# Second attention of a two-block transformer kernel: row sums from a column of ones, maxima ahead of VectorE's other work, gate products inside the last unit

## What is computed

```python
def hybrid_layer(x, ...):
    xn = rmsnorm(x, norm_mix)
    (u_rnn, u_gate, q, k_c, v_c, k_s, v_s, k_w, v_w, g_nsa, g_a, g_b) = split(xn @ w_in)
    h_a = rg_lru(causal_depthwise_conv(u_rnn, conv_w, conv_b), ...)
    y_a = h_a * gelu(u_gate)
    y_b = nsa_mixer(q, k_c, v_c, k_s, v_s, k_w, v_w, g_nsa, rel_bias, ...)
    merged = sigmoid(g_a) * (y_a @ proj_a) + sigmoid(g_b) * (y_b @ proj_b)
    h = x + merged @ w_out
    return h + square(relu(rmsnorm(h, norm_mlp) @ w_mlp_in)) @ w_mlp_out

# rg_lru: r, i = sigmoid(block-diagonal products of x); a = exp(-8 r softplus(-lam))
#         h_t = a_t h_{t-1} + sqrt(1 - a_t^2) (i_t x_t)
# nsa_mixer, each of three branches: softmax(q k + bias) v, times a gate, summed
```

## Time and profile before

| | us |
|---|---|
| median of 3 runs | 1597.65 (1597.32 to 1603.59) |
| profiled execution, its own time | 1600.37 |
| its span, first to last instruction | 1598.6 |
| TensorE busy | 1533.4 (96%) |
| VectorE busy | 1030.2 (64%) |
| ScalarE busy | 797.7 (50%) |
| GpSimd busy | 223.3 (14%) |
| mean granted clock of TensorE | 0.984 |

### The profile page before, as it was taken

How to read it: one execution, slowest core, us unless ns; L and a number is a source line. 1 busy time by engine, 2 the same in 40 slices (tenths; PEclk the granted TensorE clock), 3 DMA queues, 4 the chain that set the end, 5 groups by cost and what they waited for, 6 DMA issues and landing times.

```text
span 1598.6 us, 25010 instructions
## 1 busy us (share of the span) xinstructions
PE 1533.4 (96%) x10255; PEld 1381.4 (86%) x10255; DVE 1030.2 (64%) x1704; ACT 797.7 (50%) x1437; POOL 223.3 (14%) x189
## 2 busy tenths in 40 slices
PE   8999999999999999989999999999989799999999
PEld 6899889799987889989889987788877699989887
DVE  5764586787756675578678765555755586666643
ACT  5555454366643455445456653453446664455532
POOL 2300032211102120032031100012010050100000
PEclk9989999999999999999999999999999799999999
DMA  8623255355565533255355555555212144645453
GB/s 310 246 102 99 91 211 185 136 197 183 185 217 189 189 122 118 81 198 185 109 197 180 182 200 178 186 197 185 90 46 76 53 158 157 206 163 184 159 190 123
DMA packets 40353, 258.19 MB, mean 162 GB/s; under 512 B 4512, under 2 KB 5168, under 8 KB 14000
## 3 DMA queue, kind: packets, MB, share of 16 engines
q1 hardware_dynamic: 35600, 238.44, 42.8%
q0 software_dynamic: 2272, 12.57, 2.1%
q10 hardware_dynamic: 2368, 5.58, 0.9%
HBM read 254.98 MB, written 1.07 MB: 160 GB/s over the span
## 4 chain that ended last, share of the span: by engine, by line
PE 73%; DVE 13%; ACT 8%; issue 4%; DMA 2%; POOL 1%; ACTq 0%; POOLq 0%; DVEq 0%; SPq 0%
PE ps L492 65%; DVE lows L1557 5%; ACT wh L1037 3%; PE ps L602 3%; PE ps L683 1%; ACT S L1460 1%; DVE ar L2093 1%; PE ps L704 1%; DMA raw<-d_wst 1%; ACT arR L1538 1%; DVE S L2274 1%; DVE S L2155 1%; DVE xTr L1576 1%; PE ps L722 1%; PE ps L721 0%
## 5 line engine op out<-in xcount | busy, mean ns | idle before, releaser
L1557 DVE TENSOR_TENSOR lows<-raw,wh 128x1024 fp32r<-128x1024 f32 (+3 forms) x473 | 544.9, 1171 | 249.8 <-ACT wh L1037 247.2
L492 PE MATMUL ps<-xTr,wh 128*128 128x256 f32 (+2 forms) x3472 | 633.8, 285 | 3.4 <-DVE S L1924 1.6
L492 PEld LDWEIGHTS ps<-xTr,wh 128*128 128x128 f32 (+2 forms) x3472 | 537.9, 190 | 8.8 <-DVE S L1924 3.0
L1037 ACT CAST wh<-raw 128x1024 fp32r<-128x1024 f32 (+3 forms) x473 | 455.2, 989 | 176.6 <-DMA raw<-d_wst 131.4
L492 PE MATMUL ps<-xTr,lows 128*128 128x256 f32 (+1 forms) x1736 | 491.3, 283 | 0.0
L492 PEld LDWEIGHTS ps<-xTr,lows 128*128 128x128 f32 (+1 forms) x1736 | 330.0, 190 | 0.0
L492 PE MATMUL ps<-wh,arR 128*128 128x512 f32 x928 | 298.2, 399 | 7.4 <-DVE ar L1746 4.0
L492 PEld LDWEIGHTS ps<-wh,arR 128*128 128x128 f32 x928 | 175.1, 189 | 52.7 <-DVE ar L1746 5.7
L492 PE MATMUL ps<-lows,arR 128*128 128x512 f32 x464 | 184.1, 397 | 0.0
L492 PE MATMUL ps<-wh,xTr 128*128 128x512 f32 x480 | 153.3, 397 | 16.7 <-DVE xTr L1576 13.1
L492 PE MATMUL ps<-arR,wh 128*128 128x256 f32 (+1 forms) x832 | 148.7, 281 | 0.0
(11 more groups left out here) (259 smaller groups left out, 1514.7 us busy)
## 6 DMA issues: line engine op xcount, KB each, us to landing
raw<-d_wst SPq DMA_DIRECT2D x196, 1024.0 KB, 4.9
raw<-d_wst SPq DMA_DIRECT2D x24, 512.0 KB, 3.5
raw<-d_wst SPq DMA_DIRECT2D x12, 896.0 KB, 4.5
raw<-d_wst SPq DMA_DIRECT2D x8, 672.0 KB, 4.6
ar<-d_lnp POOLq DMA_DIRECT2D x5, 1024.0 KB, 5.2
raw<-d_wst SPq DMA_DIRECT2D x8, 441.0 KB, 3.5
ar<-d_par POOLq DMA_DIRECT2D x2, 1192.0 KB, 9.6
ar<-d_scr POOLq DMA_DIRECT2D x1, 2048.0 KB, 9.2
```

The costliest lines, as they stand in the source:

```text
L492: op = e.matmul(out, s, m, start=start and i == 0, stop=stop and i == len(pairs) - 1)
L1037: e.copy(high_of(m), raw_of(m)).then_inc(*high.done(m))
L1557: e.tensor_tensor(low_of(m), raw_of(m), high_of(m).bitcast(F32), ALU.subtract).then_inc(*low.done(m))
```

## The change

1. `vb`, the values, gets 65 columns a head (`d=65`); GpSimd sets the 65th to 1 once. `pv2` multiplies by 65 columns, and the sum of a head's probabilities comes out as the 65th column of its result. The exponentials lose their accumulator. VectorE's reciprocal and gate multiplication move from `maxima` into `finish` and read the sum from PSUM.
2. VectorE's order in a unit is now: maxima of unit un, copy of unit un − 1, finish of unit un − 2, two steps (none in unit 0). Its steps thus run one unit behind those of TensorE and ScalarE.
3. In the last unit of tile 1 TensorE runs the gate products (0, 0), (0, 1) and (0, 2) ahead of the last transposes, ahead of the last value product and behind it. ScalarE and VectorE make their halves in units 5 to 7. ScalarE takes their tanh (`gated2`) among the decays and copies that follow.
4. The square root comes behind the tanh of gate product (0, 3), the recurrences start four gate products later, and the splits of their results six iterations behind instead of two, the last two beside `pb`.

```diff
-ARENA = 25360
+ARENA = 25376
-        vb = arena(1024).rearrange("p (i c) -> p i c", i=2)
+        vb = arena(1040).rearrange("p (i h d) -> p i h d", i=2, d=65)
@@ tensor @@
+            def gate2(v, n):
+                features(("g2", v, n), W2, 8, 128, RW, span((GB0, GA0)[v] + n * 128), X, [], act, "g2", v, n)
...
+                    w.wait_ge(pool, "ones")
...
-                            v = br * 256 + h * 64
-                            op = e.matmul(b[:, h * 64:(h + 1) * 64], PTv[:, hold + h, k, :], vb[:, k, v:v + 64],
+                            op = e.matmul(b[:, h * 65:(h + 1) * 65], PTv[:, hold + h, k, :], vb[:, k, 4 * br + h, :],
...
+                if i:
+                    gate2(0, 0)
                 probs_turned(7)
                 lru_next(1)
+                if i:
+                    gate2(0, 1)
                 finish(7)
+                if i:
+                    gate2(0, 2)
@@ scalar @@
+            def gated2(v, n):
+                highs_of("g2", v, n)
+                w.wait_ge(product, "g2", v, n)
+                for k in (6, 7):
+                    w.wait_ge(cross, *(("pv2", 1, k) if v == 0 else ("pT2", 1, k, 1)))
+                e.activation((gb, ga)[v][:, n, :], M["g2", v, n][:, 0:T], ACT.Tanh, scale=0.5).then_inc(*act.done("g2", v, n))
+
+            def branch_high(k):
+                w.wait_ge(pool, "ya", k)
+                e.copy(yaR.h[0:RP, k, :], gg2[0:RP, k, :]).then_inc(*act.done("yah", k))
...
-                        op = e.activation(Sv[:, hold + h, 0:nk], Sv[:, hold + h, 0:nk], ACT.Exp, bias=nb[:, h:h + 1], scale=1.0,
-                                          accum_out=su[:, h:h + 1])
-                        op.then_inc(*act.done("exp2", i, un))
-                    lru_next(2)
+                        e.activation(Sv[:, hold + h, 0:nk], Sv[:, hold + h, 0:nk], ACT.Exp, bias=nb[:, h:h + 1],
+                                     scale=1.0).then_inc(*act.done("exp2", i, un))
+                    lru_next(1 if (i, un) == (1, 7) else 2)
+                    if i and un > 4:
+                        highs_of("g2", 0, un - 5, far=0)
                 probs_copied(7)
-                lru_next(1)
+                if i:
+                    for n in range(2):
+                        gated2(0, n)
+                lru_next(2 if i else 1)
...
+            gated2(0, 2)
             w.wait_ge(cross, "yT", 1, 1)
...
             lru_next(60)
+            gated2(0, 3)
...
+            for n in range(4, 16):
+                gated2(n // 8, n % 8)
+                if n > 5:
+                    branch_high(n - 6)
             for n in range(8):
                 highs_of("pb", n)
+                if n < 2:
+                    branch_high(10 + n)
@@ vector, maxima @@
-                    go = 16 * (br + 1) + 4 * hq
-                    w.wait_ge(act, "exp2", i, un)
-                    e.reciprocal(ri, su).then_inc(*vec.done("ri0", i, un))
-                    w.wait_ge(vec, "ri0", i, un)
-                    e.tensor_tensor(ri, ri, ng[:, i, go:go + 4], ALU.mult).then_inc(*vec.done("ri2", i, un))
@@ vector, finish @@
+                    go = 16 * (un // 4 + 1) + 4 * (un % 4)
+                    o = M["pv2", i, un][:, 0:260].rearrange("p (h d) -> p h d", d=65)
                     w.wait_ge(cross, "pv2", i, un)
+                    e.reciprocal(ri, o[:, :, 64]).then_inc(*vec.done("ri0", i, un))
+                    w.wait_ge(vec, "ri0", i, un)
+                    e.tensor_tensor(ri, ri, ng[:, i, go:go + 4], ALU.mult).then_inc(*vec.done("ri2", i, un))
...
                 for un in range(8):
+                    maxima(un)
                     if un:
                         probs_copied(un - 1)
-                    maxima(un)
+                    if un > 1:
+                        finish(un - 2)
+                    if un:
+                        lru_next(2)
+                    if i and un > 4:
+                        lows_for("g2", 0, un - 5, far=0)
+                probs_copied(7)
+                finish(6)
+                lru_next(1 if i else 3)
+                finish(7)
+                if i:
                     lru_next(2)
-                    if un:
-                        finish(un - 1)
-                probs_copied(7)
-                lru_next(1)
-                finish(7)
+                    lows_for("g2", 0, 3)
...
+            for n in range(16):
+                lows_for("g2", n // 8, n % 8)
+                if n == 4:
+                    w.wait_ge(act, "sqrt")
+                    e.memset(xc[0:RP, :, 0:1], 1.0).then_inc(*vec.done("first"))
+                if n >= 4:
+                    recur(n - 4)
+                if n > 5:
+                    branch_low(n - 6)
@@ gpsimd @@
             e.dma_start(TB, bass.AP(scr_d.tensor, 0, [[1, 128], [384, 16], [1, 256]])).then_inc(*bias_in.done())
+            e.memset(vb[:, :, :, 64:65], 1.0).then_inc(*pool.done("ones"))
```

38 lines of the change are left out of this document (11 added, 27 removed).

## The result

The changed kernel takes 1577.59 us in the median of four runs (1575.99 to 1583.21), the kernel before 1599.87 beside it (four runs); the ratio is 0.9865, with a 95% interval of 0.9831 to 0.9900. The profiled execution took 1578.58 us with a span of 1576.8, so it is 21.8 us shorter than the one of before (1598.6). Forecast were a gain of 22.4 us and a median of 1575.2. The medians differ by 22.3 us; the changed kernel's own lies 2.4 us above the forecast, and 2.2 us of that are the median of before, 1597.65 with three runs when the forecast was made and 1599.87 with four.

A forecast was written before the change was run, and what follows sets the result against it. TensorE, 96% busy, was taken to bound the kernel, with time to win only where it idles in the second attention. Gains 9.0 + 6.3 + 7.4 − 0.3 = 22.4 us off 1597.65 gave 1575.2, range 1570 to 1587.

The forecast's parts named there:

- tile 0: First attention tile: TensorE sets the pace at 7.74 us a unit; 56.0 us against 65.05, gain 9.0 us.
- boundary between the tiles: From tile 0's end to tile 1's first scores: the sum had no term; tile 0's end chain was put at 1.83 us.
- six units of tile 1: Second tile: with the maxima first, units of 6.42 us, six in 38.5 against 44.86; gain 6.3 us.
- last scores to gate product (0,7): Handover to the gate products: 23.4 us against 30.82, less four products already done; idles of 3.5 and 2.4 us; gain 7.4.
- 65th column: 192 value products with 65 columns: 0.3 us lost for all, bounds 0 and 22.
- everything behind: Recurrences, their products on GpSimd and branch splits after the handover keep their pace: nothing won or lost, ±1 us.
- rival B: Clock falls in the new idle before (0,3), which with (0,4) eats the 2.4 us spare: 1577 to 1580; chance 0.12.
- A: Loops hide less, low halves being 0.5 us from late: ten units lose 0.5 us each, 1580; chance 0.12.
- C: Handover gives nothing, ScalarE's queue from last values to square root being longer: gain 15 only, 1582.6; chance 0.09.
- D: No idle before (0,3) because casts run ahead near the square root: 3 to 5 us more, 1571; chance 0.05.
- E: Value products slowed by 65-column rows at odd multiples of four bytes: gain gone if doubled, 1619 if tripled; chance 0.03.
- F: VectorE keeps waiting, for `pv2` instead of `exp2`: 1596 or so; chance 0.04.

The follow-up runs named there:

- e1_sums: Kernel before with only the column of ones and the reciprocal behind the value product, engine order kept: 1600.24 us, ratio 0.9996 to before.
- e9_shift: e1_sums with VectorE's recurrence steps run one unit behind, maxima still after the copy: 1581.71 us, ratio 0.9878 to before.
- e10_first: e1_sums with VectorE's maxima first in each unit and finishing two units later, steps not shifted: 1588.03 us, ratio 0.9921 to before.
- e13_copyfirst: Changed kernel with VectorE's copies ahead of the maxima again and finishing one unit later, steps still shifted: 1576.71 us, ratio 0.9857 to before.
- e2_acc: Changed kernel with the exponentials' accumulators kept, 64 value columns and the reciprocal taken from those sums: 1576.49 us, ratio 0.9852 to before.
- e6_fill: Changed kernel with two unused products of constants on TensorE ahead of the transposes of tile 0's y: 1577.56 us, ratio 0.9851 to before.
- after_again: The changed kernel itself, unaltered, measured again later in six runs: 1576.74 us, ratio 0.9858 to before.
- e11_all: Changed kernel with e5_decays' edits, the cast of (0,7) directly behind the square root, and e6_fill's two products: 1570.83 us, ratio 0.9811 to before.
- e5_decays: Changed kernel with decays 9 to 11 ahead of the gate tanhs, (0,3)'s low half earlier, (0,6)'s cast ahead of the square root: 1572.79 us, ratio 0.9825.
- e4_low: Changed kernel with the low half of gate piece (0,3) made ahead of VectorE's last recurrence steps: 1579.88 us, ratio 0.9865 to before.

## Why the prediction came out right, and where it did not

Term by term, from the two profiled executions:

| term | forecast | measured |
|---|---|---|
| tile 0 | 9.0 | 65.05 − 56.25 = 8.8 |
| boundary between the tiles | 0 | 9.21 − 12.54 = −3.3 |
| six units of tile 1 | 6.3 | 44.86 − 38.52 = 6.3 |
| last scores to gate product (0,7) | 7.4 | 42.5 − 35.3 = 7.2 |
| 65th column | −0.3 | 0 |
| everything behind | 0 | 2.6 |
| rest | 0 | 0.1 |
| sum | 22.4 | 21.8 (rounded) |

**Tile 0: the sum right, its reason wrong.** 56.25 us against 56.0, units of 7.72 to 7.98 against 7.74, the end chain's idle 1.82 against 1.83. TensorE's work does set the pace, as the sum said. But the step "the change takes the wait for the exponentials off VectorE" credits the wrong edit. With that wait alone removed (e1_sums) nothing is gained, because behind it stood the cast that ScalarE makes after the same exponentials; I had both waits in the earlier trace rows, 1.71 and 0.46 us, and subtracted both without asking which edit removes the second. The one that does is the shift of the recurrence steps by a unit (e9_shift), and it makes the first one harmless too. The maxima's place with the later finishing removes a part of it alone (e10_first, 62.06 us).

**Tile 1: the same.** 38.52 against 38.5. "After the change the maxima come first" was to be the reason; e9_shift and e13_copyfirst have them second and take 38.52. By an estimate, 1 us of the 6.3 is the half clock of before at 1246.7 to 1250.1, which made its last scores late: the unit ahead of them took 8.09 us, and 7.05 in e1_sums, whose VectorE keeps the same pace. The handover's gain is smaller by as much.

**The handover: right but for one step.** (0,2) done and y transposed at 1259.17, 16.8 us after the scores, and to 17.5 with the transposes themselves; idle 3.37 against 3.5; (0,3) at 21.2 against 21.0; the square root at 29.7 against 29.8; (0,7) could start at 34.8 against 34.9, and does in e2_acc, e13_copyfirst and e6_fill. The step that went otherwise is rival B's: the clock fell in the new idle, to 0.50 in 1264 to 1268, and (0,3) and (0,4), partly at half clock, ate the 2.4 us that TensorE had to spare ahead of (0,7). In those three kernels 0.4 us of idle are left; in the changed kernel, where half clock lasted longer, none, and (0,7) came 0.5 us late, at 35.3. So B cost 0.5 us here, because the square root's chain is nearly as long. The Trainium skill's page "TensorE: Matmul & The Clock Gate", section "HAM oscillation — how this bites in real kernels", tells of a kernel whose bursts of products, with waits between them, each start at half rate; for the idles of 3.4 to 4.8 us the traces agree, six of six, and for the 1.82 us idle in six cases of eleven.

**The boundary: the step that is missing.** The sum has no term for it, though it held a new idle of 1.83 us by my own working. I had taken two idles of 1.60 us at full clock as the answer for all of that length. The trace of before had a third idle of 1.60 us in the same tile, and with that one the clock fell (TensorE's row, then the window with its clock):

```profile
1182.22 1.12 PE L602 MATMUL ps<-cst,S 128*128 128x128 f32 x4 [1.60 <-ACT S L1460]
```
```profile
1182.00:1185.00 3.00, 2.77 (x9) 0.50 0.01 3
```

That is the 0.97 of the earlier trace rows, which I had read past. The fall at the boundary cost 3.3 us in the profiled execution, TensorE being busy all the while: the transposes of y took 1.94 us in place of 1.06. It cost 1.8 us in after_again, where it lasted 6.8 us in place of 10.2.

**Behind the gates.** The changed kernel is 19.2 us ahead at (0,7), 19.2 to 19.9 at the products of the first branch and 19.9 through to 1500 us; the last 1.9 us come in the last stage, which this change does not touch. There, both kernels have the same stall, and only before's execution fell in clock behind it; first before (1502 to 1512), then changed (1480 to 1490):

```profile
1502.00:1512.00 10.00, 7.64 (x26) 0.83 0.32 107
```
```profile
1480.00:1490.00 10.00, 7.65 (x38) 1.00 0.31 107
```

after_again has that fall (0.66 in 1484 to 1488), so it goes with the execution and not with the kernel; of the fourteen profiled executions twelve have it, all but changed and e11_all. Across it before loses 1.6 us to changed. That this offsets half of the loss at the boundary is luck, and it is why 22.4 and 21.8 lie so near; without the 3.3 and the 1.9 us the changed kernel would be 23.2 us ahead.

**The rivals.** A happened in small, in two of tile 0's units, which take 7.87 and 7.98 us. The low half and the product that needs it, VectorE and TensorE:

```profile
1164.00 1.08 DVE L1579 TENSOR_TENSOR lows<-raw,wh 128x896 fp32r<-128x896 f32 x1
```
```profile
1165.23 0.46 PE L492 MATMUL ps<-xTr,wh 128*112 128x256 f32 x2
```

The half is there at 1165.08, 4.0 us after the unit's scores (1161.07) and not the 3.4 of the sum, and the product is some 0.2 us late. e9_shift and e13_copyfirst, which finish a unit behind the low halves, have 7.72 us in these units and tile 0 in 55.84 and 55.85: A costs 0.4 us, not 5. C and D did not: the handover measured as worked out. D's idea, casts and decays further ahead, was there to be had, and e5_decays and e11_all have it: 1572.8 and 1570.8. E fell with the 1.82 us of 16 products. F, that VectorE keeps waiting, is what the first part does when it is alone, for a cast and not for `pv2`.

## What to carry to other kernels

When a wait is to be removed, read what the same engine waits for next, and from whom: if the next operation depends on something that the releasing engine does behind the old releaser, only the name of the wait changes (1.71 + 0.46 us became 2.17). What empties such a loop is distance, running the steps that ping between two engines one unit behind, so that each finds the other's part done; here that one moved call took 18.5 us off the medians (1600.24 to 1581.71). The maxima's place with the later finishing took 12 off alone and nothing beside the shift, the column nothing. And when an idle stretch is removed, look for the chain right behind it: e4_low moved 3.4 us of idle time to another place, e5_decays removed it.

## What the runs showed of the hardware

- The same instructions with the same idle of 1.82 us kept the whole clock in five profiled executions and lost half of it for 7 to 10 us in six, at 1.8 to 3.3 us of cost (11.0 to 12.5 us from the transposes of y to tile 1's first scores, against 9.2). Of three idles of 1.60 us in tile 0 of before, one went with a fall. A kernel's executions differ by 4 to 11 us, and in most kernels the longer ones have the lower mean clock (e13_copyfirst: 1574.82 us at 0.991, 1583.97 at 0.984), though not in e2_acc (1576.25 at 0.992, 1575.78 at 0.990); that the falls make most of the spread is likely and not shown.
- A value product of 65 columns costs what one of 64 does, 0.114 us, though its rows start at odd multiples of four bytes.
- Reading the accumulator is an instruction of its own behind each exponential (1437 instructions before, 1373 after); without it the next one of 256 columns follows after 0.40 us instead of 0.49, and the kernel did not feel it.
